# The h buffers of a hybrid transformer kernel with rows 784 columns apart instead of 772

## What is computed

```python
for l in range(DEPTH):                       # DEPTH = 2
    mod = silu(c) @ w_ada[l] + b_ada[l]      # shift, scale, gate for mixer and for FFN
    mod_c = silu(c_ctx) @ w_ada[l] + b_ada[l]
    h  = rmsnorm(x, g_mix[l]) * (1 + sc1) + sh1
    hc = rmsnorm(ctx, g_mix[l]) * (1 + csc1) + csh1
    q, k, v, u = split_in(h @ w_in[l])       # rotary on q and k
    # the same for hc; in the last layer only its k and v
    a_out  = latent_attention(q, k, v, k_c, v_c, attn_sink[l])   # window +-128, and all context keys
    cv_out = silu(layernorm(depthwise_conv31(u[:, :512] * sigmoid(u[:, 512:]))))
    x = x + gt1 * (concat([rmsnorm(a_out), rmsnorm(cv_out)]) @ w_out[l])
    h2 = rmsnorm(x, g_ffn[l]) * (1 + sc2) + sh2
    x = x + gt2 * (silu(h2 @ w_gate) * (h2 @ w_up)) @ w_down     # D_FF = 2816
    # context tokens: the same in layer 0, nothing more in layer 1
return rmsnorm(x, g_final)
```

## Time and profile before

| | |
|---|---|
| time, median of 3 runs | 1590.11 us |
| the profiled execution | 1588.25 us |
| its span, first to last instruction | 1586.4 us |
| mean granted TensorE clock | 0.991 of full speed |
| TensorE matmuls busy (PE) | 1533.7 us, 97% of the span, 9714 matmuls |
| weight loads (PEld) | 1274.5 us, 80% |
| VectorE (DVE) | 936.5 us, 59% |
| ScalarE (ACT) | 536.9 us, 34% |
| GpSimd (POOL) | 128.4 us, 8% |
| the chain that ended last, by engine | PE 86%, DVE 6%, ACT 4%, issue 2% |

### The profile page before, as it was taken

The page is one execution under the profiler, slowest core; times in us unless marked ns, Lnnn a source line. Parts: engine busy times, 40 slices in busy tenths (PEclk is TensorE's granted clock), DMA queues, the critical chain, the costliest instruction groups (busy, mean ns, idle before and its releaser), DMA issues.

```text
span 1586.4 us, 24584 instructions
## 1 busy us (share of the span) xinstructions
PE 1533.7 (97%) x9714; PEld 1274.5 (80%) x9714; DVE 936.5 (59%) x1571; ACT 536.9 (34%) x858; POOL 128.4 (8%) x163
## 2 busy tenths in 40 slices
PE   6999998999999999999999999998999999999996
PEld 3865764688888888888888888676679998998995
DVE  2584689767666325765654466678786443443445
ACT  3312378724222112221122243148844222322222
POOL 0033221040000000000000001511020000000000
PEclk9999999999999999999999999999999999999998
DMA  9582600012333223333522123410022332323222
GB/s 358 207 242 58 241 12 27 1 54 107 119 122 103 67 81 144 119 115 123 191 74 62 54 70 108 137 54 1 28 67 93 93 93 93 93 93 95 93 87 83
DMA packets 39865, 161.16 MB, mean 102 GB/s; under 512 B 5616, under 2 KB 6000, under 8 KB 33648
## 3 DMA queue, kind: packets, MB, share of 16 engines
q1 hardware_dynamic: 35856, 148.72, 27.6%
q0 software_dynamic: 3936, 11.45, 2.6%
HBM read 149.76 MB, written 2.10 MB: 96 GB/s over the span
## 4 chain that ended last, share of the span: by engine, by line
PE 86%; DVE 6%; ACT 4%; issue 2%; POOL 1%; DMA 1%; SPq 0%; DVEq 0%; ACTq 0%; POOLq 0%
PE banks L496 74%; PE banks L525 3%; PE banks L613 2%; PE banks L433 1%; PE banks L640 1%; PE banks L625 1%; POOL z_padded L1528 1%; DVE row_max L1132 1%; PE banks L677 1%; PE banks L465 1%; ACT prob L819 1%; PE banks L483 1%; ACT w_high L736 1%; DMA ada_first<-in_w_ada 1%; ACT probT L831 1%
## 5 line engine op out<-in xcount | busy, mean ns | idle before, releaser
L496 PE MATMUL banks<-h_high,w_high 128*128 128x512 f32 (+1 forms) x1856 | 433.0, 314 | 3.9 <-DVE w_low L1015 2.4
L496 PE MATMUL banks<-h_high,w_low 128*128 128x512 f32 (+1 forms) x1856 | 427.8, 312 | 0.0
L496 PE MATMUL banks<-h_low,w_high 128*128 128x512 f32 (+1 forms) x1856 | 426.5, 311 | 0.0
L736 ACT ACTIVATE w_high<-raw 128x1024 fp32r<-128x1024 f32 (+1 forms) x178 | 185.3, 1041 | 697.0 <-PE banks L496 677.7
L496 PEld LDWEIGHTS banks<-h_high,w_high 128*128 128x128 f32 x1856 | 288.0, 189 | 38.3 <-issue 14.6
L1015 DVE TENSOR_TENSOR w_low<-raw,w_high 128x1024 fp32r<-128x1024 f32 (+1 forms) x178 | 216.3, 1215 | 171.1 <-ACT w_high L736 167.5
L496 PEld LDWEIGHTS banks<-h_low,w_high 128*128 128x128 f32 x1856 | 287.7, 189 | 21.1
L496 PEld LDWEIGHTS banks<-h_high,w_low 128*128 128x128 f32 x1856 | 286.4, 189 | 20.6
L1059 DVE COPY shift_product<-banks 128x2 f32<-128x2 f32 x116 | 18.4, 159 | 310.1 <-PE banks L496 299.2
L496 PE MATMUL banks<-ff_high,w_high 128*128 128x512 f32 (+1 forms) x528 | 160.5, 358 | 0.6 <-DVE ff_low L1389 0.6
L496 PE MATMUL banks<-ff_high,w_low 128*128 128x512 f32 (+1 forms) x528 | 159.6, 357 | 0.0
(11 more groups left out here) (171 smaller groups left out, 1623.5 us busy)
## 6 DMA issues: line engine op xcount, KB each, us to landing
raw<-in_w_gu SPq DMA_DIRECT2D x88, 512.0 KB, 3.5
ada_raw<-in_w_ada SPq DMA_DIRECT2D x21, 1024.0 KB, 5.7
raw<-in_w_dn SPq DMA_DIRECT2D x32, 512.0 KB, 3.5
raw<-in_w_mix SPq DMA_DIRECT2D x28, 512.0 KB, 5.0
ada_in_ff<-in_w_ada SPq DMA_DIRECT2D x12, 1024.0 KB, 5.5
raw<-in_w_out SPq DMA_DIRECT2D x16, 512.0 KB, 3.5
ada_first<-in_w_ada SPq DMA_DIRECT2D x7, 1024.0 KB, 14.1
raw<-in_w_dn SPq DMA_DIRECT2D x16, 384.0 KB, 3.0
```

Of the source, the lines that this page charges most:

```text
L496: last = mm(bank[:, 2 * slot + bk, 0:b - a], weights[w][:, k0_w + k, :], rhs[:, k0_rhs + k, a:b], start=(k == 0 and n == 0), stop=(k == kt ...
L736: f(wH[j][:, 0:k, :], raw[j][:, 0:k, :], ACT.Copy).then_inc(w_high, 1)
```

## The change

`HC`, the column at which the context begins, goes from 514 to 520, and `HW`, the columns of a row, from 772 to 784. The number of columns that a matmul reads, and all else, stays. A row has 3136 bytes (24 x 128 + 64), so row k begins at a multiple of 128 for even k and 64 bytes behind one for odd k; the context piece begins 2080 bytes further (16 x 128 + 32).

The spare columns (514 to 519 and 778 to 783) are neither written nor read. `h_low` begins 384 bytes later than before; what lies behind it (`z_padded`, `conv`, `k_stacked`, `q_stacked`, `ff_high`, `ff_low` and the others) moves by 768 bytes, and `attn_out` by 192. But for `attn_out`, which goes from 64 bytes behind a multiple of 128 to a multiple, a buffer's start keeps its place within 128 bytes. No instruction is added, taken away or moved on any engine.

```diff
-HC = N + 2
-HW = HC + L + 2
+HC = N + 8
+HW = HC + L + 8
@@ mod_cols
-            return [(0, 0, N), (1, HC, HW)] if context else [(0, 0, N // 2), (1, N // 2, HC)]
+            return [(0, 0, N), (1, HC, HC + L + 2)] if context else [(0, 0, N // 2), (1, N // 2, N + 2)]
@@ shift_high (ScalarE) and shift_low (VectorE)
-                for at in (N, HW - 2):
+                for at in (N, HC + L):
```

## The result

The changed kernel takes 1593.58 us (median of 7 runs, 1591.03 to 1595.62), the kernel before in the same comparison 1589.21 us (1587.55 to 1590.46). The ratio is 1.0029, 95% interval 1.0019 to 1.0039: slower by 0.29%. The profiled execution took 1593.04 us with a span of 1591.2 us, 4.8 us more than before, at the same mean granted clock of 0.991.

The account below looks back on a forecast made before the run. TensorE's matmuls were taken to bound the kernel. The profiled 1588.25 us + 1.1 + 0 made 1589.35, or 1591.2 us against the median; own range 1588 to 1594 us, 8-in-10 range 1580 to 1600.

Parts of the forecast that it names:

- TensorE carries the cost to the end: In phases where TensorE is full, each nanosecond per matmul reaches the end; 825 us of matmuls have changed addresses.
- The place of a row shows in the time: In h, k-steps starting at different places within 128 bytes take slightly different times, 1.04 to 1.06 us.
- addresses do nothing: Rival: uneven k-steps come from position in the block, so time stays 1590.1 us; chance 0.09.
- (a): 1440 matmul pairs of h with context: +0.75 ns a pair, +1.1 us, the middle between ff and conv.
- upper bound: For h with context: ff's excess of 13.3 ns a pair, +3.4 ns a pair or +4.9 us.
- even placing: Rows all starting at one place in 128 bytes: best within one bank, worst when pieces alternate between two, 13.3 ns excess.
- (b): 1344 matmul pairs of h without context: no change, 0 us.
- the floor: Rate of evenly placed ff matmuls without context: 226.7 ns for 512 columns, 0.4427 ns a column.
- (c): Writes of h by VectorE, 746 ns in the mean for 512 columns: no change, 0.
- (d): Buffers moved by 768 bytes, and attn_out: no change, 0; ff, attn and conv streams keep their times.
- locks in a bad rhythm: Rival in TensorE's pairs over two banks: even placing adds +9.1 us, giving 1599.2 us; slower by over 3.2 us had 0.28.
- The reading of ff as a matter of banks: In ff with context, the 13.3 ns excess a pair was put on evenly placed pieces alternating between two banks.

Follow-up runs that it names:

- e10: Kernel before with layer 1's down projection in two pieces of 256 columns over two banks instead of one of 512: 1595.57 us, ratio 1.0048.
- e7: Kernel before with the rows of w_high and w_low 132 columns apart instead of 128: 1593.88 us, ratio 1.0030.
- e3: Changed kernel with the two inner loops of tile_product exchanged, three products of one piece before those of the next: 1592.31 us, ratio 1.0016.
- e8: Changed kernel with the rows of h_high alone 800 columns apart, h_low staying at 784: 1593.68 us, ratio 1.0034.
- e9: Kernel before with the four weight tiles moved 128 bytes later, data buffers keeping their place within 256 bytes: 1590.32 us, ratio 1.0013.
- e6: Changed kernel with h_low 64 bytes later; its two pads also moved ff, attn and conv by 128 bytes: 1597.86 us, ratio 1.0053.
- e4: Kernel before with the two inner loops of tile_product exchanged: 1588.62 us, ratio 1.0000.
- e2: Kernel before with the context piece at column 520 and rows 780 columns apart: 1588.23 us, ratio 0.9992.
- e11: Kernel before with h_low 128 bytes later, at the same place within 256 bytes as h_high: 1588.43 us, ratio 0.9996.

## Why the prediction was right, and where it was off

- *TensorE carries the cost to the end.* Right: +5.2 us from the blocks, +4.8 us in the span.
- *The place of a row shows in the time.* Right: every layout of h in the table changed the block with context or the one without, by 7 to 73 ns, where e10 with h unchanged repeats both lengths; the rival "addresses do nothing" is out. The Trainium skill (page "TensorE: Matmul & The Clock Gate", section "Back-to-back issue gap") gives the gap of a lone matmul from the column count alone. For a stream of weight loads and matmuls the same section says that both set the spacing, without a term for the address. In e7 a matmul of the same shape in the same stream takes 232.5 in place of 226.7 ns, so the column count alone does not set it here. (The prediction took the full clock from the earlier trace rows for the matmuls of the earlier trace rows, which run later; from 1549 to 1552 us the granted clock is 1.00 too.)
- *(a) h with context, +1.1 us.* The value was mis-sized: +4.5 us, near the upper bound (-2.7 to +4.9). I had taken the middle between ff and conv, and the changed rows came out with an excess of 13.0 ns, close to the 13.3 of ff. The bounds held, but the reason for them did not: they rested on even placing being the worst for two banks, and e3, e8 and e9 speak against that. That the result landed between them is in part luck. The overall range held 1593.58 us because it took in the upper bound, and the forecast's own range (1588 to 1594) held it only just.
- *(b) h without context, 0.* Near: +0.7 us. The gain down to the floor didn't come, and e10 shows why it was not to be expected: evenly placed short pairs take 240.0 ns, not 226.7.
- *(c) and (d), nothing.* Right: 749 against 746 ns, ff at 353.3 and 226.7 ns. The move by 768 bytes is three times 256; e6 shows that 128 bytes would not have been free.
- *The likeliest class.* I gave 0.38 to no change (within 3.2 us), 0.28 to slower. The result is slower by 4.4 us, 0.29%. What happened is the rival "locks in a bad rhythm" in its place and with half its price: 4.4 us of the 9.1, nearly all with context. My test for it (four blocks over 34.0 us) was just missed by 33.98. Its reason, even placing, is not shown: e8 places `h_high` more evenly and changes nothing with context.
- *What the profile would show.* I expected k-steps to be alike for k two apart. They are alike for k four apart: I had counted places within 128 bytes, and the k-steps tell rows apart that lie 128 bytes off.
- *The reading of ff as a matter of banks.* Wrong: e3 and e4 change the bank in one matmul of three. The block with context gets 67 ns shorter in one and 27 longer in the other, and neither kernel is faster than before. The floor is no fixed rate either: the same stream of 512-wide matmuls takes 226.7 or 233.3 ns (e9). The excess needs another explanation.

One bound of (a) was also misread. The 348.0 ns of a conv pair with context came from 10 pairs, which is no whole number of k-steps. The conv k-steps repeat after four of them, 12 pairs, and those take 4.20 us here, 350.0 ns a pair (349 in the two earlier conv stretches):

```profile
338.53 0.51 PE L496 MATMUL banks<-conv_high,w_high 128*128 128x512 f32 x2
...
342.73 0.51 PE L496 MATMUL banks<-conv_high,w_high 128*128 128x512 f32 x2
```

So the excess of conv is 9 to 10 ns, that of h itself, and not 8.0. The lower bound would have been -1.3 to +0.1 us in place of -2.7, and the middle +1.8 to +2.5 us in place of +1.1. The measured +4.5 us is still near the upper bound.

What stays open: by what mechanism the places of data and weights change the length. ff pairs at the same addresses settled at 353.3 ns in some stretches of the runs e2, e8 and e11 and at 346.7 in others, so addresses alone don't fix the length. What came before in the stream may take part, which no run here varies alone. No formula here gives a block's length from its layout.

## What to carry to other kernels

Where TensorE is full for hundreds of microseconds, the layout of its operands is worth some tenths of a per cent, with no instruction changed; read it from start-to-start times over whole loop bodies, since the page's mean durations and busy shares barely show it (314, 312 and 311 ns before, 314, 313 and 312 after; 97% in both). "Aligned" is no direction, and the place of the weights counts as well as that of the data, so try a few row distances and starts, and compare block lengths in one profile each before timing any. Bound such a change by other streams of the same kernel, and take no value inside the bounds as likelier than the rest: with one pattern of pieces, h with context took from 8393 to 8493 ns a block.

## What was not expected of the hardware

- Block lengths come in steps of 6.67 ns: 8420, 8413.3, 8466.7, 8473.3, 8493.3 with context, 5693.3, 5700, 5706.7, 5720 without. In each run but e7, about nine in ten or more of the stretches of eight k-steps with no other matmul in them take the same time to 1 or 2 ns. In e7 most of them spread between about 8440 and 8505 ns with context.
- Moving all weights by 128 bytes (e9) and moving the ff data by 128 bytes (e6) give the same two numbers in the stretches shown, 350.8 and 233.3 ns, in place of 353.3 and 226.7: one got shorter and the other longer.
- The fastest block with context (8393 ns) came from moving weights, not data. That kernel lost it again in ff (233.3 ns a matmul), and none of the twelve beats the kernel before beyond its interval.
